# A hybrid diffusion step on one core: expert stores awaited by their gathers, last norm rows loaded early, second mixer's queries and keys projected in turned form

## The reference

```python
h = x * (1.0 + sc1) + sh1
qa, ka, va, qb, kb, vb, qc, kc, vc = jnp.split(h @ w_in_l, _in_offsets(), axis=-1)
...
y = (ga * (oa @ w_br_l[0]) + gb * (ob @ w_br_l[1]) + gc * (oc @ w_br_l[2])) @ w_o_l
x = _layernorm(alpha * x + g1 * y, ln_g_l[0], ln_b_l[0])
h2 = x * (1.0 + sc2) + sh2
m = _moe(h2, w_router, router_bias, moe_w1_l, moe_w3_l, moe_w2_l)
return _layernorm(alpha * x + g2 * m, ln_g_l[1], ln_b_l[1])
```

## Time and profile before

| | |
|---|---|
| median of three runs | 2271.79 us (2268.26 to 2272.42) |
| the profiled execution's own time | 2269.82 us |
| its span | 2267.7 us |
| TensorE busy (PE) | 2115.3 us, 93% |
| VectorE (DVE) | 1083.0 us, 48% |
| ScalarE (ACT) | 519.6 us, 23% |
| GpSimd (POOL) | 236.7 us, 10% |

### The profile page before, as it was taken

How to read it: one execution, slowest core, us unless ns; L and a number is a source line. 1 busy time by engine, 2 the same in 40 slices (tenths; PEclk the granted TensorE clock), 3 DMA queues, 4 the chain that set the end, 5 groups by cost and what they waited for, 6 DMA issues and landing times. The chain is left out here.

```text
span 2267.7 us, 26885 instructions
## 1 busy us (share of the span) xinstructions
PE 2115.3 (93%) x10730; PEld 1376.2 (61%) x10730; DVE 1083.0 (48%) x1701; ACT 519.6 (23%) x992; POOL 236.7 (10%) x272
## 2 busy tenths in 40 slices
PE   6999999999999998899689999999999999969991
PEld 3457754576567654788544676447756775458880
DVE  1135457243444364664242453745434444865434
ACT  2014301242134200122130341113402440012221
POOL 1000010020100000211110001002101000011113
PEclk8999999999999999899899999999999999979996
DMA  8121166311110325899760111642111105159985
GB/s 335 44 78 38 48 217 227 112 52 60 56 40 32 159 104 222 293 370 359 259 221 37 61 38 61 223 172 82 45 60 58 38 20 232 40 188 361 362 323 176
DMA packets 59439, 334.64 MB, mean 148 GB/s; under 512 B 8704, under 2 KB 9696, under 8 KB 30192
## 3 DMA queue, kind: packets, MB, share of 16 engines
q1 hardware_dynamic: 33408, 238.70, 29.0%
q0 software_dynamic: 15008, 56.96, 7.6%
q10 hardware_dynamic: 10896, 37.23, 4.2%
HBM read 300.47 MB, written 35.01 MB: 148 GB/s over the span
## 5 line engine op out<-in xcount | busy, mean ns | idle before, releaser
L808 PE MATMUL ps<-ring,hT 128*128 128x512 f32 (+1 forms) x1280 | 530.5, 570 | 1.9 <-issue 1.9
L808 PE MATMUL ps<-hT,ring 128*128 128x320 f32 x1536 | 464.3, 440 | 0.0
L808 PEld LDWEIGHTS ps<-ring,hT 128*128 128x128 f32 x1280 | 239.8, 191 | 253.6 <-issue 246.8
L808 PEld LDWEIGHTS ps<-hT,ring 128*128 128x128 f32 x1536 | 272.8, 190 | 97.3 <-issue 1.6
L808 PEld LDWEIGHTS ps<-zT,ring 128*128 128x128 f32 x2176 | 254.1, 194 | 18.4 <-issue 15.3
L808 PE MATMUL ps<-zT,ring 128*128 128x128 f32 x2176 | 258.5, 278 | 2.3 <-ACT zT L1483 2.3
L808 PE MATMUL ps<-R,ring 128*128 128x512 f32 (+1 forms) x768 | 211.1, 435 | 4.6 <-DVE zT L1795 3.2
L1430 ACT COPY R<-ps 128x512 f32<-128x512 f32 (+2 forms) x170 | 96.2, 566 | 383.8 <-PE ps L1021 381.6
L808 PEld LDWEIGHTS ps<-R,ring 128*128 128x128 f32 x768 | 116.9, 191 | 98.6 <-issue 92.5
L808 PE MATMUL ps<-ring,zT 128*128 128x512 f32 x320 | 139.0, 593 | 0.0
L1662 DVE SCALAR_TENSOR_TENSOR R<-ring,cs,R 128x2048 f32<-128x2048 f32 x56 | 131.7, 2352 | 5.8 <-DMA ring<-in_wall 4.0
(11 more groups left out here) (237 smaller groups left out, 1954.2 us busy)
## 6 DMA issues: line engine op xcount, KB each, us to landing
ring<-in_wall SPq DMA_DIRECT2D x224, 1024.0 KB
y_rows<-R ACTq DMA_DIRECT2D x34, 512.0 KB, 9.6
R<-in_rows POOLq DMA_DIRECT2D x2, 4096.0 KB, 15.3
R<-mrows POOLq DMA_DIRECT2D x16, 512.0 KB, 17.8
R<-in_x ACTq DMA_DIRECT2D x10, 512.0 KB, 8.5
h_rows<-R ACTq DMA_DIRECT2D x10, 512.0 KB, 2.7
R<-in_bias POOLq DMA_DIRECT2D x8, 384.0 KB, 4.1
x_state<-R POOLq DMA_DIRECT2D x1, 2560.0 KB, 9.8
```

The source lines that it names most:

```text
L808: ins = nc.tensor.matmul(out, w, m, start=start, stop=stop, **kw)
```

## The change

It does three things.

1. The second mixer's queries and keys (chunks 3 and 4) are projected turned: the weights are stationary, 320 tokens of hT move, and the result lies as `QT` and `KT` want it. A chunk has eight units (four blocks of 128 columns by two halves of the tokens) instead of five, ScalarE copies each unit straight to its place (queries with the scale), and the transposes of these units and their second copies are gone. The keys of the context tokens are stored from `KT`, in another layout of the output, in pieces of 512 bytes. The first modulation group is added up behind unit (4, 1) instead of (4, 0).
2. At a layer's end ScalarE doesn't wait for its stores; their two semaphores are outside the set that the barrier clears and count on through both layers, and GpSimd waits for them in front of its gathers. VectorE's gate operation goes ahead of its wait for TensorE's result.
3. The last norm's rows are loaded by SyncE behind the last expert's pieces, into an area that is free then. In the last block VectorE sums two tiles ahead.

```diff
-MOD_SUMS = ((4, 0), (5, 3))
+MOD_SUMS = ((4, 1), (5, 3))
...
+def stores(layer, e, n):
+
+    return layer * len(range(n, NB, 2)) + len(range(n, e, 2))
+
...
+def turned(c):
+
+    return c in (3, 4)
+
+
+def units(c):
+
+    return 8 if turned(c) else NT
...
-        rowsF = area(0, 2048).rearrange("p (a n) -> p a n", a=2)
+        rowsF = area(24064, 2048).rearrange("p (a n) -> p a n", a=2)
...
-        def fetch_and_scale(pool, ch):
-
+        def fetch_and_scale(pool, ch, layer):
+
+            for n in range(2):
+                pool.wait_ge(y_out[n], 16 * stores(layer, NB, n))
             for t in range(4):
                 fetch_outputs(pool, t)
...
-        def gate_output(ch, e, w, s):
+        def slot_gates(ch, e):
 
             ch.step(nc.vector.scalar_tensor_tensor(gsel[e % 2], G2[:, 1, :], in_ctx[:, 0, e:e + 1], gsel[e % 2], ALU.mult, ALU.add), v_chain)
+
+        def keep_gated(ch, e, w, s):
+
             ch.step(nc.vector.scalar_tensor_tensor(ysb[:, e % 2, :], flat(4, 1024), w, gsel[e % 2], ALU.mult, ALU.mult), s)
...
+                    if last_layer:
+                        sp.dma_start(rowsF[:], A["last_rows"]).then_inc(last_rows_in, 16)
...
+                            if typ == "k" and turned(c):
+
+                                pool.wait_ge(a_copy, AU.index(PU.index((br, c, units(c) - 1))) + 1)
+                                pool.dma_start(OUT["bk"][layer].rearrange("p (b t) -> p b t", b=4), KT[:, :, LTOK:TOK]).then_inc(new_k_out, 16)
+                                pool.wait_ge(new_k_out, 16 * (br + 1))
...
+                                    if turned(c):
+                                        b, part = divmod(t, 2)
+                                        last = mm(ps[:, bank_of(i), 0:320], wk[:, 128 * b:128 * b + 128], hT[:, k, 320 * part:320 * part + 320],
+                                                  k == 0, k == KB - 1, frees=k < KB - 1)
+                                        continue
...
+                                    elif turned(c):
+                                        b, part = divmod(t, 2)
+                                        dst, src = (QT if c == 3 else KT)[:, b, 320 * part:320 * part + 320], ps[:, bank_of(i), 0:320]
...
-                    for s in range(2):
-                        act.wait_ge(y_out[s], 16 * len(range(s, NB, 2)))
...
                         dve.wait_ge(a_gsel, e + 1)
+                        slot_gates(ch, e)
                         dve.wait_ge(pe_e, e + 1)
-                        if e >= 2:
-                            dve.wait_ge(y_out[e % 2], 16 * (e // 2))
-                        gate_output(ch, e, slot_w[:, e, e:e + 1] if e < NE else extra_w[:, NE:NE + 1], v_y)
+                        if stores(layer, e, e % 2):
+                            dve.wait_ge(y_out[e % 2], 16 * stores(layer, e, e % 2))
+                        keep_gated(ch, e, slot_w[:, e, e:e + 1] if e < NE else extra_w[:, NE:NE + 1], v_y)
...
+                def centred(t):
+
+                    ch.step(nc.vector.scalar_tensor_tensor(x[:, t, :], x[:, t, :], lnst[:, t, 14:15], rowsF[:, 0, :], ALU.add, ALU.mult), v_chain)
+
                 def scaled(t):
 
-                    ch.step(nc.vector.scalar_tensor_tensor(x[:, t, :], x[:, t, :], lnst[:, t, 14:15], rowsF[:, 0, :], ALU.add, ALU.mult), v_chain)
...
-                dve.wait_ge(rows_in, 16)
+                dve.wait_ge(last_rows_in, 16)
+                summed(0)
                 for t in range(NT):
-                    summed(t)
-                    if t:
-                        variance(t - 1)
-                        scaled(t - 1)
-                variance(NT - 1)
-                scaled(NT - 1)
+                    if t == 0:
+                        summed(1)
+                    variance(t)
+                    centred(t)
+                    if t + 2 < NT:
+                        summed(t + 2)
+                    scaled(t)
```

More of the change, by code:

```diff
@@ L310, in build_kernel @@
         y_init = ctx.enter_context(nc.semaphore("output_rows_filled"))
+        y_out = [ctx.enter_context(nc.semaphore(f"expert_outputs_stored_{n}")) for n in range(2)]
+        last_rows_in = ctx.enter_context(nc.semaphore("last_rows_loaded"))
         full = [sem(f"piece_loaded_{s}") for s in range(SLOTS)]
@@ L338, in build_kernel @@
         g1_in, g_in, g2_in = sem("first_gate_loaded"), sem("modulation_rows_loaded"), sem("second_gate_loaded")
-        h_out, y_out = [sem("expert_inputs_stored_0"), sem("expert_inputs_stored_1")], [sem("expert_outputs_stored_0"), sem("expert_outputs_stored_1")]
+        h_out = [sem("expert_inputs_stored_0"), sem("expert_inputs_stored_1")]
+        extra_out = sem("extra_outputs_stored")
         xg_in = [sem(f"tokens_gathered_{s}") for s in range(3)]
@@ L376, in count @@
                 return self.n.get(s.num, 0)
-        PU = [(br, c, t) for br in range(3) for c in CHUNKS[br] for t in range(NT)]
+        PU = [(br, c, t) for br in range(3) for c in CHUNKS[br] for t in range(units(c))]
         def bank_of(i):
@@ L387, in out_bank @@
             return (i + 2) % 4
-        QU = [i for i, (br, c, t) in enumerate(PU) if CHUNK_TYPE[c] != "v"]
+        QU = [i for i, (br, c, t) in enumerate(PU) if CHUNK_TYPE[c] != "v" and not turned(c)]
         def by_dve(c, t):
@@ L402, in follows @@
             return i > 0 and i - 1 in QU and PU[i - 1][0] == br and i + 1 < len(PU)
-        NEW_K = [i for i, (br, c, t) in enumerate(PU) if t == CTX and CHUNK_TYPE[c] in ("k", "kv")]
+        NEW_K = [i for i, (br, c, t) in enumerate(PU) if t == CTX and CHUNK_TYPE[c] in ("k", "kv") and not turned(c)]
         def item(br, i):
@@ L637, in _ @@
                         pool.wait_ge(y_init, 16 * len(range(1, EXTRA, 4)))
-                        fetch_and_scale(pool, ch)
+                        fetch_and_scale(pool, ch, layer - 1)
                     def powers(dst, src):
@@ L698, in _ @@
                                 if typ == "k":
-                                    pool.dma_start(OUT[("ak", "bk")[br]][layer], tok[:, q % 2, 0:512]).then_inc(new_k_out, 16)
+                                    pool.dma_start(OUT["ak"][layer], tok[:, q % 2, 0:512]).then_inc(new_k_out, 16)
                                 else:
@@ L890, in project @@
                                 transpose_x(0, 4)
-                            for t in range(NT):
+                            for t in range(units(c)):
                                 i = PU.index((br, c, t))
@@ L964, in scores @@
                         if i == 0:
-                            pe.wait_ge(a_qk, 10 * (br + 1))
+                            pe.wait_ge(a_qk, 20 if br == 2 else 10)
                             pe.wait_ge(a_copy, len([a for a in AU if PU[a][0] <= br]))
@@ L1339, in project @@
                     def project(br):
+                        if br == 2:
+                            act.wait_ge(new_k_out, 32)
                         for c in CHUNKS[br]:
-                            for t in range(NT):
+                            for t in range(units(c)):
                                 i = PU.index((br, c, t))
@@ L1369, in project @@
                                         dst, src = tok[:, q % 2, :], ps[:, bank_of(i), :]
-                                    if c != 6:
+                                    if c == 3:
+                                        ch.step(nc.scalar.activation(dst, src, ACT.Copy, scale=HD ** -0.5), a_copy)
+                                    elif c != 6:
                                         ch.step(nc.scalar.copy(dst, src), a_copy)
@@ L2078, in _ @@
                             act.wait_ge(v_y, 1)
-                            act.dma_start(A["y_rows"][NE + j], ysb[:, 0, :]).then_inc(y_out[0], 16)
-                            act.wait_ge(y_out[0], 16)
+                            act.dma_start(A["y_rows"][NE + j], ysb[:, 0, :]).then_inc(extra_out, 16)
+                            act.wait_ge(extra_out, 16)
                         @block.vector
@@ L2099, in _ @@
                             dve.wait_ge(a_gsel, 1)
+                            slot_gates(ch, NE)
                             dve.wait_ge(pe_e, 1)
-                            gate_output(ch, NE, extra_w[:, NE:NE + 1], v_y)
+                            dve.wait_ge(y_out[NE % 2], 16 * stores(layer, NB, NE % 2))
+                            keep_gated(ch, NE, extra_w[:, NE:NE + 1], v_y)
                     nc.all_engine_barrier(sems_to_clear=all_sems)
@@ L2109, in _ @@
             def _(sp):
-                sp.dma_start(rowsF[:], A["last_rows"]).then_inc(rows_in, 16)
                 for t in range(NT):
@@ L2118, in _ @@
                 ch = Chain(pool)
-                fetch_and_scale(pool, ch)
+                fetch_and_scale(pool, ch, DEPTH - 1)
                 pool.dma_reset(all_sems)
```

4 lines of the change are left out of this document (2 added, 2 removed).

## The result

The changed kernel takes 2255.07 us (median of 6 runs, 2253.54 to 2257.76) against 2270.29 (6 runs, 2267.14 to 2272.43): a ratio of 0.9934, with 0.9921 to 0.9947 as its 95% interval. That is 15.2 us less, where 16.8 were forecast from the profiled execution. The changed kernel's profiled execution has a time of 2253.54 us and a span of 2251.6, 16.1 under the span of before.

The account below looks back on a forecast made before the run. TensorE, busy 93% of the span, was taken as the bound, except at the layer ends. Turning 8.2, layer ends 7.0 and tail 1.6 sum to 16.8 us: 2269.82 to 2253.0, as a median 2255.0; range 2250.5 to 2263.5.

Parts of the forecast that it names:

- Part 1: Second mixer's projection: turned queries and keys drop the transposes, saving 4.1 us a layer, 8.2 us for two.
- Rival 3: Turned units: switches or bank waits cost 0.26 us in each of 32 units, losing the 8.2 us; 2263.2, chance 0.10.
- rival 4: Turned units: weight loads come out from under the passes, 36.5 us, making it slower at 2291.5; chance 0.04.
- Part 2: Both layer ends: gate operation moved ahead and ScalarE's store wait removed, 3.5 us each, 7.0 for both.
- Step (a): Last expert of a layer: VectorE's gate operation ahead of its wait for TensorE brings the store 1.31 us earlier.
- step (b): Layer end: ScalarE no longer waits for the store before the barrier and leaves behind its issue, 2.3 us earlier.
- Step (c): Layer end: GpSimd waits for the store before its gathers, met with 0.5 us to spare; two waits priced at 0.1 us.
- Rival 2: Layer ends: the store's landing stays on the path, each end gives 1.3 instead of 3.5 us; 2259.4, chance 0.08.
- The restart: TensorE's half-clock restart after the first layer's barrier: taken as zero, up to 2 us either way.
- Part 3: Tail, last norm: early rows and sums two tiles ahead gain 1.6 us, bounds -0.5 and 2.6.
- Landing: 24.3 to 26.4: Tail: us from the first gather until the fifth tile's second gather lands, with up to 2.1 more coming back.
- Rival 1: Tail: GpSimd's power keeps losing to VectorE, fifth pair as late as before, tail gives nothing; 2256.6, chance 0.12.

Follow-up runs that it names:

- turned_only: Changed kernel keeping only the turned queries and keys and the later modulation sum, layer ends and tail as before: 2262.46 us (5 runs), ratio 0.9964.
- four_parts: Changed kernel with the turned chunks in sixteen units of 160 columns each instead of eight of 320: 2257.48 us.
- gate_behind: Changed kernel with VectorE's gate operation again behind its wait for TensorE's result: 2258.00 us.
- store_waited: Changed kernel with ScalarE again waiting for its stores before the block ends, GpSimd waiting too: 2259.53 us.
- after: The profiled execution of the changed kernel, with nothing further changed: 2253.54 us, span 2251.6.
- double_store: Changed kernel with each layer's last slot rows stored twice, the second time to a spare place, gathers waiting for both: 2254.07 us.
- late_rows: Changed kernel with the last norm's rows loaded in the last block again, beside the gathers, new order kept: 2253.79 us.
- fifth_first: Changed kernel with all five tiles' gathers issued before GpSimd's first power in the last block: 2254.14 us (5 runs), ratio 0.9925.

## Why the prediction came out right, step by step

The forecast was 2255.0 and the time is 2255.07, but so close it came by luck: the gain was 15.2 us and not 16.8, and the median of before is 2270.29, 1.5 under that of the three runs which the forecast started from. Step by step, against the 16.1 us of the two spans:

**A reading to correct.** "TensorE stands still at the two layer ends only" says too much. Of the 152.4 us in which TensorE is idle before, the two ends have 71.3 (23.3 ahead of its restart, 48.0 behind its last result) and the first 76 us have 17.6; the rest is spread over both layers. No term of the sum rests on it.

**Part 1, right.** 8.2 forecast, 8.3 in the trace, 8.3 in turned_only's times. A pass has 270 ns, as in the earlier trace rows, in both layers. TensorE's sum came at 354.45 for the 355.2 of the text. Rival 3 (turning buys nothing) falls with turned_only, rival 4 (loads exposed, 88 ns each or more) with the 2.5 ns of four_parts, and rival 5 (saved and given back) with the times of both.

**Part 2, right mechanism, one term mis-sized.** 3.5 a layer end forecast, 2.9 and 3.0 measured. Step (a) holds: 1.31, and 1.3 in gate_behind. The term that was mis-sized is step (b), "After, ScalarE leaves behind the issue (0.34 us): 2225.0 - 2222.70 = 2.3 us". ScalarE did leave so, but the register loads that stand between its block and the barrier took longer under the store, and the barrier's clearing came 0.5 to 0.6 us later behind them (1.2 us for 0.7 in the second layer, 1.4 for 0.8 in the first); net, 1.7 and 1.8 in store_waited. I had carried the barrier's length over as a constant. GpSimd's two waits were priced at 0.1 us; store_waited, which has them, is 0.07 and 0.13 longer than before from the product to the gather. Step (c) holds: in after the gathers wait for the barrier, not for the store, and double_store shows some spare. Rival 2 falls with store_waited, where the landing on ScalarE's path costs 1.7 and 1.8 us again.

**The restart, right.** Priced at zero with 2 us either way. From the first gather to the second layer's projection it is 293.60 us for 293.82 before.

**Part 3, mis-sized, and the bounds held.** Forecast 1.6, with -0.5 and 2.6 as bounds; 1.1 to 1.2 in the profiled execution, and about 0.5 as a mean over the kernels. The step that failed is the choice inside "Landing: 24.3 to 26.4": the fifth tile's second gather started 2.1 us earlier, as I had allowed, at 17.9 us instead of 20.0, but then took 8.3 us to land, not 7.2, and the sum began at 26.3, the late end of my interval. In four other executions it was later still, up to 27.9. I had carried the 7.2 us over as if a landing followed its issue alone; the DMA engines are busy all the time up to it (a share of 1.01 in after), so it need not. The early rows, from which I had taken 0.8 us for that issue, moved no end in late_rows: the fifth pair went out 0.8 us later there (16.8 for 16.0) and was in earlier. Rival 1 (the fifth pair as late as before) falls: the pair starts 1.1 and 2.1 us earlier. GpSimd's powers do still take 1.57 us in after, but the fifth tile's landing is what VectorE waits for, and fifth_first, with most powers as long, has no wait.

**What was not in the sum.** 0.83 us of the span came from the clock between 38 and 50 us, which the change doesn't touch. It makes up for most of the 1.0 us missed at the layer ends, so the profiled execution looks nearer to the forecast than its parts are.

## What to carry to other kernels

When a wait is taken off an engine in front of a barrier, read what stands between that wait and the barrier: work that used to run after the transfer now runs beside it, and may take longer. When two chains end close together, as VectorE's work and the fifth tile's landing do here, a gain on one of them is capped by the other; find the second one's date first, and move both, as fifth_first does. Look at the DMA engines' share as well: where it is full, an earlier issue need not be an earlier landing. And count stretches between marks that both traces have: single times of this kernel hid 3 us of noise in its first 76 us, while the long stretches that the change doesn't touch agreed to 0.3 us.

## What the runs showed of the hardware

- A register load from an SBUF tile took 0.27 to 0.55 us when the last expert store had landed (before, store_waited) and 0.55 to 1.16 us while it is under way (after, double_store; five engines, two layers). Twice the bytes in flight did not make it longer than once.
- A weight load of these chunks is recorded with 190 ns at passes of 512, 320 and 160 columns, also where passes follow each other every 136 ns (four_parts). So the recorded 190 ns is not the time that a load keeps the next one waiting.
- A gather's issue on GpSimd grows beside VectorE: 1.56 to 1.58 us alone, 2.28 in fifth_first and 2.59 in late_rows beside a sum of VectorE with two inputs. In late_rows the issue starts 1.16 us before the sum's end and takes 1.0 longer; in fifth_first 0.86 before it, and takes 0.7 longer. The Trainium skill, SBUF — State Buffer, section Who interferes with whom, says that an operation of VectorE with two SBUF inputs contends with a GpSimd instruction that reads SBUF, under an exclusive lock. The gather's issue reads its row numbers (yrow) there, and these two agree; that it is this read which waits is not shown.
- The landing of the same gather varied by more than its issue, which in these kernels came 17.9 to 18.7 us behind the first gather: the fifth tile's sum began 25.6 to 27.9 us behind the first gather in kernels with the same tail.
